# Keeping the residual stream by features: square sums by products with ones, output and down weights stationary

## The reference

```python
def _rmsnorm(x, w, eps=1e-6):
    return x * lax.rsqrt(jnp.mean(x * x, axis=-1, keepdims=True) + eps) * w

# first block, DEPTH = 2
for l in range(DEPTH):
    sh1, sc1, g1, sh2, sc2, g2 = split(silu(c) @ ada_w[l] + ada_b[l], 6)
    h = _rmsnorm(x, norm_mix_w[l]) * (1 + sc1) + sh1
    x = x + g1 * _mixer(h, ...)          # ends with merged @ w_out, 1024 x 1024
    h = _rmsnorm(x, norm_ffn_w[l]) * (1 + sc2) + sh2
    x = x + g2 * _conv_ffn(h, ...)       # D_FF = 2816
return _rmsnorm(x, final_norm_w)

def _conv_ffn(h, w_up, conv_w, conv_b, w_down):
    u = _causal_dwconv(h @ w_up, conv_w, conv_b)      # 3 taps over tokens
    a, val = jnp.split(u, 2, axis=-1)
    return (gelu(a) * val) @ w_down
```

## Time and profile before

| | |
|---|---|
| median of 3 runs | 2029.18 us (2027.23 to 2029.62) |
| profiled execution, span | 2031.2 us (no other time is recorded for it; 2.0 over the median) |
| instructions | 31646 |
| busy: PE / PEld / DVE / ACT / POOL | 91 / 77 / 79 / 53 / 7% of the span |
| mean read from HBM | 226 GB/s |
| opening ends | 33.3 us |
| mixer 0, FFN 0 | to 293.1, to 498.6 us |
| mixer 1, FFN 1 | to 754.7, to 960.5 us |
| second stage | to 1194.8 us |
| second output, experts | from 1385.4, from 1441 us |

### The profile page before, as it was taken

The page is one execution under the profiler, slowest core; times in us unless marked ns, Lnnn a source line. Parts: engine busy times, 40 slices in busy tenths (PEclk is TensorE's granted clock), DMA queues, the critical chain, the costliest instruction groups (busy, mean ns, idle before and its releaser), DMA issues. The chain is left out here.

```text
span 2031.2 us, 31646 instructions
## 1 busy us (share of the span) xinstructions
PE 1852.5 (91%) x12866; PEld 1571.9 (77%) x12866; DVE 1605.9 (79%) x2103; ACT 1086.4 (53%) x1306; POOL 145.0 (7%) x151
## 2 busy tenths in 40 slices
PE   2989989999989989999999868998899999999998
PEld 2876769997866769997877657876788788787786
DVE  6777888987788888987579487647788888887887
ACT  2643536653653627562564423125577677676675
POOL 0000000000000000000056047300000000000000
PEclk9989999999999999999999978998899999999999
DMA  7566766656567756556521100006599899898997
GB/s 278 209 221 236 258 207 259 239 203 226 195 215 250 265 188 271 226 198 233 186 73 63 60 12 15 19 16 254 183 369 376 318 372 368 324 375 309 337 373 289
DMA packets 158288, 460.54 MB, mean 227 GB/s; under 512 B 11072, under 2 KB 13760, under 8 KB 155584
## 3 DMA queue, kind: packets, MB, share of 16 engines
q1 hardware_dynamic: 158144, 458.52, 62.7%
HBM read 457.43 MB, written 1.05 MB: 226 GB/s over the span
## 5 line engine op out<-in xcount | busy, mean ns | idle before, releaser
L217 DVE TENSOR_TENSOR me_wlow<-me_w,me_whigh 128x2048 fp32r<-128x2048 f32 (+1 forms) x203 | 451.9, 2248 | 87.4 <-ACT me_whigh L212 87.1
L212 ACT ACTIVATE me_whigh<-me_w 128x2048 fp32r<-128x2048 f32 (+1 forms) x203 | 380.4, 1886 | 138.8 <-PE ps L225 122.9
L223 PE MATMUL ps<-me_whigh,me_xhigh 128*128 128x512 f32 x512 | 206.0, 402 | 5.1 <-PEq L124 3.1
L225 PE MATMUL ps<-me_whigh,me_xlow 128*128 128x512 f32 x528 | 207.6, 393 | 0.0
L223 PE MATMUL ps<-up_xhigh,ffn_whigh 128*128 128x256 f32 x704 | 199.8, 284 | 2.6 <-DVE ffn_wlow L217 1.5
L224 PE MATMUL ps<-me_wlow,me_xhigh 128*128 128x512 f32 x512 | 201.2, 393 | 0.0
L224 PE MATMUL ps<-up_xlow,ffn_whigh 128*128 128x256 f32 x704 | 199.2, 283 | 0.0
L225 PE MATMUL ps<-up_xhigh,ffn_wlow 128*128 128x256 f32 x704 | 199.2, 283 | 0.0
L217 DVE TENSOR_TENSOR ffn_wlow<-ffn_w,ffn_whigh 128x2048 fp32r<-128x2048 f32 (+1 forms) x72 | 149.3, 2111 | 43.2 <-ACT ffn_whigh L212 43.0
L217 DVE TENSOR_TENSOR mix_wlow<-mix_w,mix_whigh 128x1024 fp32r<-128x1024 f32 (+2 forms) x116 | 140.2, 1211 | 23.6 <-ACT mix_whigh L212 23.6
L212 ACT ACTIVATE ffn_whigh<-ffn_w 128x2048 fp32r<-128x2048 f32 (+1 forms) x72 | 123.4, 1763 | 43.1 <-PE ps L225 43.1
(11 more groups left out here) (678 smaller groups left out, 4162.8 us busy)
## 6 DMA issues: line engine op xcount, KB each, us to landing
me_w<-w_exp_gate SPq DMA_DIRECT2D x34, 2048.0 KB, 10.0
me_w<-w_exp_up SPq DMA_DIRECT2D x34, 2048.0 KB, 10.4
me_w<-w_exp_down SPq DMA_DIRECT2D x32, 2048.0 KB, 10.2
mix_w<-w_mix SPq DMA_DIRECT2D x108, 512.0 KB, 4.1
mix_ada_w<-ada_w SPq DMA_DIRECT2D x96, 512.0 KB, 4.5
ffn_w<-ffn_w_up SPq DMA_DIRECT2D x20, 2048.0 KB, 7.8
ffn_w<-ffn_w_down SPq DMA_DIRECT2D x8, 2048.0 KB, 8.7
sec_w<-w_in SPq DMA_DIRECT2D x31, 512.0 KB, 3.8
```

What stands on the lines that cost most here:

```text
L212: return nc.scalar.activation(high, x, ACT.Copy)
L217: return nc.vector.tensor_tensor(low, x, high.bitcast(F32), ALU.subtract)
L223: nc.tensor.matmul(out, lh, rh, start=start, stop=False)
L225: return nc.tensor.matmul(out, ll, rh, start=False, stop=stop)
```

## The change

- x and the context are turned on the host and kept by features, [128, 8, 256], up to the experts. There 16 transposes and 4 copies make `x_tok` by tokens, in `second_output`.
- A norm is: 8 squares (ACT, 128x256), 8 fp32 products with a 128x128 matrix of ones over 256 columns, all into one bank, which gives each token's sum on every partition; root (ACT) and reciprocal (DVE, 128x256); then per feature tile x times gain times root (DVE), plus shift, to the high part (ACT), and the low part (DVE). No diagonal, no turning products. The squares and sums stand at the end of the stage before (mixer, FFN, opening), as does the reciprocal for mixer 0.
- With features on the partitions the gates g1 and g2 are one value per partition: the residual is a single operation per feature tile, out of PSUM. The spreads are gone (g2's row for the experts stays).
- Out and down products have the weights stationary: 192 of 128x256 for each 96 of 128x512, 528 for each 264. Two feature tiles share a bank in the out products, with one `core.clear` (a product of zeros, 512 columns) for each of the four banks. The down products use all eight banks and wait for all low parts of a chunk first.
- The opening loads x between the sixth and seventh of its eight transfer pairs. The mixer's planned first piece goes from 11 to 7, fills are 0 in mixer 0, 30 in mixer 1 (as before) and in the FFNs (12, and 6 and 14 in the first chunk, before).
- The FFN's first chunk goes feature tile by feature tile over its four units.
- In the last layer the FFN also sums squares weighted with the final norm's gain. From both sums the second stage makes the root of its latent norm at once; x itself is scaled by the final norm later (planned at 25.8). The broadcast row is a column of 8. `pieces.clock` goes from 16 to 8, fills from 90 to 40, and the pieces' order becomes f0, f1 (tile by tile, together), rw0, rw1, rw8, f2 to f5, vg, rw 6, 7, 2 to 5, nq, nk, nv.

The core of the diff:

```diff
+    def clear(self, bank):
+        self.nc.tensor.matmul(bank, self.zeros[:, 0:P], self.zeros[:, P:3 * P].unsqueeze(1).to_broadcast([P, 2, 2 * P]),
+                              start=True, stop=False)
...
+def inverse_root(core, sem, what, sums, rstd, at):
...
+        nc.scalar.activation(rstd, sums, ACT.Sqrt, bias=core.eps, scale=1.0 / DM).then_inc(rooted, 1)
...
+        dve.wait_ge(rooted, 1)
+        nc.vector.reciprocal(rstd, rstd).then_inc(made, 1)
...
+def normed_features(core, sem, what, x, gain, shift, rstd, ready, hT, xs, at):
...
+        for kt in range(KD):
+            yield at + 0.45 + 0.84 * kt
+            act.wait_ge(scaled, kt + 1)
+            nc.scalar.activation(xs[0][:, kt, :], hT[:, kt, :], ACT.Identity, bias=shift[:, kt:kt + 1]).then_inc(x_high, 1)
...
+            if kt < KD:
+                nc.vector.scalar_tensor_tensor(out=hT[:, kt, :], in0=x[:, kt, :], scalar=gain[:, kt:kt + 1], in1=rstd,
+                                               op0=ALU.mult, op1=ALU.mult).then_inc(scaled, 1)
+            if kt:
+                dve.wait_ge(x_high, kt)
...
```

Opening:

```diff
+                    if j == x_at:
+                        sp.dma_start(x[:, :, :], x_from).then_inc(x_here, 16)
...
+                    if i == NEXT - 2:
+                        dve.wait_ge(rooted, 1)
+                        V.reciprocal(rstd, rstd).then_inc(inverted, 1)
```

Mixer, out products and residual:

```diff
-                    for t in range(TT):
-                        if kq == 0:
-                            units.read(pe, before_out[2 * c + t])
-                        mm = tokens(f"out{c}{t}", mT, w, 2, 2 * kq, 512, t, kq == 0, kq == 3, out_units)
+                    for d in range(KD // 2 * c, KD // 2 * (c + 1)):
+                        b, col = divmod(d, 2)
+                        out = out_units.bank(f"out{b}")
+                        if kq == 0 and col == 0:
+                            units.read(pe, before_out[b])
+                            core.clear(out)
+                        n0 = P * (d % (KD // 2))
+                        for n in range(2):
+                            mm = split_product(nc, out[:, SEQ * col:SEQ * (col + 1)], [kview(a, 2)[:, n, n0:n0 + P] for a in w],
+                                               [a[:, 2 * kq + n, :] for a in mT], False, kq == 3 and col == 1 and n == 1)
...
+                ins = nc.vector.scalar_tensor_tensor(out=x[:, d, :], in0=out_units.bank(f"out{b}")[:, SEQ * col:SEQ * (col + 1)],
+                                                     scalar=mod[:, 2 * KD + d, 0:1], in1=x[:, d, :], op0=ALU.mult, op1=ALU.add)
```

FFN, first chunk and down products:

```diff
+            for kt in range(KD):
+                pe.wait_ge(x_low, kt + 1)
+                if kt in starts:
+                    pe.wait_ge(low, 1 + starts.index(kt))
+                for n in range(2 * pairs):
+                    up_product(n, kt)
...
+                for i in starts:
+                    pe.wait_ge(low, before(n) + 1 + starts.index(i))
+                for q in range(KD // 2):
+                    d = KD // 2 * c + q
                     for i in range(kn):
-                        if t == 0 and i in starts:
-                            pe.wait_ge(low, before(n) + 1 + starts.index(i))
-                        mm = split_product(nc, down_bank(c, t), [a[:, k0 + i, t * P:(t + 1) * P] for a in hid],
-                                           [a[:, n % STAGES, i, :] for a in parts], k0 + i == 0, k0 + i == FF_TILES - 1)
+                        mm = split_product(nc, down_bank(d), [a[:, n % STAGES, i, q * P:(q + 1) * P] for a in parts],
+                                           [a[:, k0 + i, :] for a in hid], k0 + i == 0, k0 + i == FF_TILES - 1)
...
+                        if c == 1:
+                            for s in ((0, 1, 2, 3), (4,), (5,))[q]:
+                                add_square(pe, s)
```

Second stage:

```diff
-        pieces.clock = 16.0
+        pieces.clock = 8.0
+        for name, order, costs in (("f", (0, 1), {0: 3.3, 1: 3.3}), ("rw", (0, 1, 8), {0: 3.3, 1: 3.3, 8: 3.3}),
+                                   ("f", (2, 3, 4, 5), {}), ("vg", range(4), {i: 4.5 for i in range(4)}),
+                                   ("rw", (6, 7, 2, 3, 4, 5), {}),
...
+            nc.vector.tensor_scalar(rstd[:, 1, :], x_sums[0], EPS, EPS * EPS * DM, ALU.mult, ALU.add).then_inc(final_own, 1)
+            dve.wait_ge(final_own, 1)
+            nc.vector.tensor_tensor(rstd[:, 1, :], rstd[:, 1, :], x_sums[1], ALU.add).then_inc(final_own, 1)
```

More of the change, by code:

```diff
@@ L1008, in mixer @@
         units = Units(core, sem, "mix", banks, names)
-        out_names = [f"out{c}{t}" for c in range(2) for t in range(TT)]
+        out_names = [f"out{b}" for b in range(banks)]
         before_out = names[-banks:]
@@ L1812, in mixer, with square_act @@
+        def square_act(act):
+            for d in range(KD):
+                yield out_at(d) + 0.5
+                act.wait_ge(res_made, d + 1)
+                nc.scalar.activation(squares[:, d, :], x[:, d, :], ACT.Square).then_inc(squared, 1)
         with nc.Block(no_gpsimd_drain=True) as block:
@@ L2045, in main_act @@
                 split(n)
-            nc.scalar.activation(rstd[:, 0:1], k["ones"][:, 0:1], ACT.Sqrt).then_inc(table_ahead, 1)
+            if final is not None:
+                act.wait_ge(final_here, 16)
+            for d in range(KD):
+                square(d)
+                if d == KD // 2 - 1:
+                    nc.scalar.activation(ahead, k["ones"][:, 0:1], ACT.Sqrt).then_inc(table_ahead, 1)
         def main_dve(dve):
-            yield 13.0
-            order, down_order = Order(dve, up_own), Order(dve, down_own)
+            yield 10.5
+            order = Order(dve, up_own)
             def split(n):
@@ new lines, in context_act, with context_pe @@
+        def context_act(act):
+            for kt in range(KD):
+                yield 4.0 + 0.84 * kt
+                act.wait_ge(ctx_here, 16)
+                nc.scalar.activation(ctx_sq[:, kt, :], xc[:, kt, :], ACT.Square).then_inc(ctx_squared, 1)
+        def context_pe(pe):
+            yield 0.0
+            core.fill(core.ps[:, 7, :], 40)
+            for kt in range(KD):
+                yield 9.6 + 0.01 * kt
+                pe.wait_ge(ctx_squared, kt + 1)
+                mm = nc.tensor.matmul(ctx_sums, k["ones"], ctx_sq[:, kt, :], start=kt == 0, stop=kt == KD - 1)
+            mm.then_inc(ctx_summed, 1)
@@ new lines, in add_square, with ended @@
+        def add_square(pe, d):
+            pe.wait_ge(squared, max(d + 1, 2))
+            mm = nc.tensor.matmul(sums, ones, squares[:, d, :], start=d == 0, stop=d == KD - 1)
+            if d == KD - 1:
+                mm.then_inc(summed, 1)
+        def ended(d):
+            return 3 + d // 2 + 1
+        def rows_dve(dve):
+            yield 0.0
+            nc.vector.scalar_tensor_tensor(out=gain, in0=mod[:, 4 * KD:5 * KD, 0], scalar=1.0, in1=fv["norm2"],
+                                           op0=ALU.add, op1=ALU.mult).then_inc(gained, 1)
+            yield 15.5
+            nc.vector.tensor_tensor(diag[:, :, :], ident.unsqueeze(1).to_broadcast([P, KD, P]),
+                                    mod[:, 5 * KD:6 * KD, 0].unsqueeze(2).to_broadcast([P, KD, P]), ALU.mult)\
+                .then_inc(row_made, 1)
```

759 lines of the change are left out of this document (346 added, 413 removed).

## The result

The changed kernel takes 2067.3 us in the median of 4 runs (2064.2 to 2071.3), the kernel before 2029.0 us (2027.2 to 2029.6): a ratio of 1.0188, 95% interval 1.0171 to 1.0205. The forecast was 2019.3, so the sign was wrong and the time lies outside the range (2008 to 2030).

What follows compares the result with a forecast made beforehand. The prediction took PE, busy 91%, as the bound, with movable time in the seams. Terms 0.2 + 2.5 + 15.7 − 11.6 + 2.6 − 3.0 + 2.5 + 1.0 = +9.9 off 2029.2 gave 2019.3 us, range 2008 to 2030.

Steps and rivals of the forecast that it cites:

- Step 9: Second stage (S is a stage's starting barrier): first products at S+12, f5 done at S+51.8 against S+53.0; +2.5 us gained.
- a stage bound by PE: Rival: PE bounds the second stage, so +9.4 us counts there instead of +2.5, total 2012; chance 0.15.
- The bound for f2: Second stage: where f2 waits for the context's norm, up to 2 us are lost.
- Step 2: Square sums in mixers and FFNs: 0.22 us per product; −0.9 per mixer, −1.3 in FFN 0, −2.6 in FFN 1.
- Step 10: Second output: first product some 2 us earlier, −2.15 for halved products and clears, norm some 10.5 instead of 12; +1.0 us.
- Step 8: Opening and mixer 0: barrier about 4.2 us later, first product at S+8.7, cold start −1.0; together −3.0 us.
- Step 5: FFN starts: first product near S+8.2, first chunk ends at S+19.9; +7.7 us in layer 0, +8.0 in layer 1.
- Step 1: Out and down products halved to 256 columns at 0.120 us each: −3.5 us per layer down, −1.3 per out projection.
- the rival of the weight load: Loading stationary tiles sets the spacing of halved out and down products: 117 us more, or 33 in part; chance 0.02.
- Step 7: Start of mixer 1: first product at S+8.5, latent part bound by the pieces until S+19.4; +2.6 us.
- Step 4: Seams behind the mixers: some 2.4 us after the last out product; +1.0 us in layer 0, +1.5 in layer 1.
- The rival of the cold starts: At six stage starts the low clock falls on real products, 2.8 us each, 17 in all, total 2036; chance 0.10.

Runs made afterwards that it cites:

- e1_sec: Changed kernel with the second stage's weight splits planned later (from 13, piece clock 15 instead of 8), context's squares at 10.4 and root at 12.9: 2058.2 us.
- e5_order: e1_sec with the second stage's pieces back in the order of the kernel before (rw0, rw1, rw8 last): 2055.1 us.
- e9: e8_all_warm with the second stage's pieces in the order of before and the opening's reciprocal four tiles earlier: 2033.8 us.
- e4_ones: Changed kernel with the square sums of opening, mixers, FFNs and context in float32r instead of float32: 2066.1 us.
- e11_left: e3_out with seven of the eight products with ones left out of the second output: 2070.9 us in one run.
- e10: e9 with second output changed: square sums behind out products, 12 products of zeros, logits by feature tile, route behind two of four turning groups: 2026.8 us.
- e3_out: Changed kernel, second output only: spread of g2 behind the transposes of x, third low part of expert weights ahead of the last residuals: 2065.5 us.
- e2_open: Changed kernel, opening only: x loaded behind the second of eight transfer pairs instead of the sixth: 2069.1 us.
- e6_warm: Changed kernel with more products of zeros before first real ones: mixer 0 from 0 to 60, mixer 1 30 to 70, FFNs 30 to 58: 2076.7 us.
- e8_all_warm: Changed kernel with e1_sec, e2_open, e3_out and e4_ones together, plus the products of zeros of e6_warm: 2041.1 us.
- e7: Changed kernel with e1_sec, e2_open, e3_out and e4_ones together, without the added zeros of e6_warm: 2055.6 us.

## Why the prediction was wrong, point by point

**Step 9, the second stage (forecast +2.5, measured −17.8): the step that failed.** Two things in it. "Weights land 9 late, so first products at S+12, norm steps to S+20" took the norm to run beside the transfer. I worked out what each operation costs and not what stands in front of it: the first product came at S+20.8. The S+12 was out of reach in any order, since the trace of before has the first split of these weights only at S+13.4 (from `second_vectors`), when they have landed, and high and low part take 2.3; no version came under S+19.3.

```profile
974.31 1.06 ACT L212 ACTIVATE sec_whigh<-sec_w 128x1024 fp32r<-128x1024 f32 x1 [2.28 <-DMA sec_w<-w_in]
```

As for the order, the planned time of the pieces went from 16 to 8, their splits with it, and ACT runs its queue in order, so the first split's wait for its transfer (15.43) became the root's wait, and held both norms. e1_sec takes that away: −9.9, by way of the context's norm. The 9.4 for a stage bound by PE was also a slip, 31.2 − 21.4 is 9.8. And the bound for f2, "up to −2", was far too near: f2 waited for the context's norm, whose sums stood behind f0 and f1 on PE, while 72 other products stood ahead of it: S+48.2 instead of the forecast's S+30.0. e5_order gives 6.0 more. With both the stage is within 1.9 us of before, with e9 3.2 under it. That the stage's time goes by f2 was right, and it made every us of f2's delay count: from f2 to the end there are 200.4 to 206.0 us in the ten traces without the long low stretch, 212.5 to 215.1 in the three with it.

**Step 2, square sums: a price of half the true one (part 2 of the prediction).** I read "24 products take 2.84" off a row whose count is of records. The turning products of a norm appear as 32 records, and there are 16 in the code (8 feature tiles times 2), not 32 as I had put it; a float32 product is two records. The spread of the gate has 8 products, in 16 records. So 0.43 us each, not 0.22: for the six in the flow FFN 0 −2.6 instead of −1.3, for the twelve FFN 1 −5.2 instead of −2.6. e4_ones shows the difference in both FFNs. In the mixers it is not the price that counted but the wait for the squares: four sums hold up the out products for 2.8 and 2.3 us, where I had 0.9. The Trainium skill, "FP8 and Floating Point Precision", section "TensorE Precision Notes", has true FP32 as four passes through the array. The measured 0.43 against 0.12 us for 256 columns in float32r is 3.6 times, which is near it.

**Step 10, second output (+1.0, measured −12.5).** The sum had only durations (and its terms, 2 − 2.15 + 1.5, make +1.35). The first product did not start 2 sooner: the first clear waited 2.92 for a low part of the weights and came 0.4 sooner than the first product before. The 7.2 us in the flow of the out products are 2.4 of dearer products and clears, some 3.8 of four sums and the waits for squares, and about 1 of the low clock at the start; e11_left shows the wait for squares, whose residuals stand behind expert weights on DVE. Taking the sums out of the flow (e10) does not bring the last sum forward, so it is the residuals and not PE's queue that set it. The other 5.6 are the tail: DVE's 2.28 inside the norm, the logits at the low clock, the route behind 28 records. Of the 12.5, e3_out recovers 2.9 and e10 seven in all. Before, the norm ran by token tile, the first tile's beside the second tile's products; by features it can only start when all eight tiles are there. That this is the rest of the loss (5.4 in e10) is argued, not shown.

**Step 8, opening and mixer 0 (−3.0; −6.4 by the end of mixer 0).** The barrier came 6.5 later, 2.3 more than forecast, by the wait for the root that I had left out; e2_open takes 2.4 of it back. The first product at S+8.8 was right to 0.1. The cold start cost 2.4 instead of 1.0. The rest of the 6.4 belongs to this one execution: with the same code up to there, e3_out ends mixer 0 at 294.0, 0.9 behind before, and not at 299.4. The terms of this part also don't add up as written: 4.2 later and a first product 1.2 sooner are −3.0 before the cold start, where I put −2.0.

**Step 5, the FFN's start: right.** First product at S+7.1 (forecast 8.2; S+8.9 in layer 1), the first chunk's last product at 319.31, S+19.9 (forecast 19.9); in layer 1 at S+21.9. The gain of 7.7 and 6.1 is there:

```profile
319.31 0.28 PE L230 MATMUL ps<-up_xhigh,ffn_wlow 128*128 128x256 f32 x1
```

With the sums at their true price FFN 0 should come to 7.7 − 3.5 − 2.6 = +1.6, and was +1.0; FFN 1, with the 0.7 for its tail, to 6.1 − 3.5 − 5.2 − 0.7 = −3.3, and was −3.3.

**Step 1, halved products: right.** 0.119 to 0.120 in down, at the out products 0.12 where the clock is full; so the rival of the weight load is out. (A clear at the 512-column spacing is 0.227, where I took 0.21; on four of them that is nothing.)

**Step 7, mixer 1 (+2.6, measured 0 at the end of the latent part).** The first product was at S+8.5 as forecast, but ran at the low clock: the last wide latent product starts at S+21.8, where it was S+21.9. In e6_warm it starts at S+19.5, the forecast's S+19.4. **Step 4, the seams,** came out as forecast within 1 us (mixer 0: 2.6 us from the last out product to the first fill, forecast 2.4).

**The rival of the cold starts** had its place right in four stages (clock 0.80 to 0.88 over the first products). Against the starts at 1.00 in e6_warm and e8_all_warm the products there took 2.4 us more in each mixer, 1.4 and 1.6 in the FFNs, 8 us and not 17. It made no more than a fifth of the result, and what I had not seen is that the clock's largest effect sits in no stage's start but at the end of the second one: 11 to 12 us, counted from f2, between versions that have the same code there. The latent products here are 0.281 apart on average in a start at a clock of 0.81 and 0.230 in e6_warm at 1.00. The first of them, at the lower level, stand 0.43 apart in the timeline of PE after:

```profile
49.10 0.63 PE L229 MATMUL ps<-mix_wlow,mix_xhigh 128*128 128x512 f32 x1
49.53 0.63 PE L230 MATMUL ps<-mix_whigh,mix_xlow 128*128 128x512 f32 x1
49.96 0.63 PE L228 MATMUL ps<-mix_whigh,mix_xhigh 128*128 128x512 f32 x1
```

The Trainium skill, "TensorE: Matmul & The Clock Gate", section "Back-to-back issue gap", gives the gap of a single product as N/1.2 ns cold and N/2.4 + 2.5 ns warm: 427 and 216 for 512 columns. The 0.43 agrees, the 0.230 is 6% over it.

## What to carry to other kernels

A planned order of queues is part of every edit: when a stream of weights is planned earlier, look at what waits for its transfer on an in-order engine and which small operation stands behind it. Cost a new operation from a row whose count you have checked against the code. Before a gain at the head of a stage is booked, find the product from which the stage's chain starts; here only its time counted (200 to 206 us from f2 to the end, whatever stood ahead). And one trace of a stage is one draw: mixer 0 differed by 5 us between traces of the same code.

## What the runs showed of the hardware

- A float32 product leaves two records and takes 0.43 us for 256 columns; in float32r it is one record of 0.12.
- The end of the second stage (PE busy 71 to 81%, in many small pieces) runs at a mean clock of 0.83 to 0.93 in ten of the thirteen traces and of 0.74 to 0.76 in three (e4, e6, e7), though its code is that of another version with the higher clock. In the three it runs 27.3 us on end at the lower level. It costs 11 to 12 us, counted from f2. What decides it stays open; PE's work in the 23 us ahead of the fall is the same in e7 and in e8, which does not fall.
- 60 products of zeros ahead of a stage's first product took 2.4 us off its first 48 wide ones, without delaying them (mixer 0, S+8.7). 70 in mixer 1 delayed them from S+8.6 to S+10.5 in e8 and e10 and not in e6; 58 in FFN 0 delayed its first product by 1.2 and saved 1.4.
